# Moving the last 24 gathered dot products from the routing's expert layer into the second expert layer, and spreading the others over the routing

## The reference, cut to what matters

```python
def block(xb):
    qy = (xb @ w_query).reshape(n_tok, PEER_HEADS, 2, half)
    s1 = einsum('nhd,hkd->nhk', qy[:, :, 0], sub_keys_1)      # 8 heads, 128 keys each side
    s2 = einsum('nhd,hkd->nhk', qy[:, :, 1], sub_keys_2)
    v1, i1 = top_k(s1, 16)
    v2, i2 = top_k(s2, 16)
    cand = v1[..., :, None] + v2[..., None, :]
    cidx = i1[..., :, None] * 128 + i2[..., None, :]
    top_s, pos = top_k(cand, 16)                               # 16 experts per head and token
    eidx = take_along_axis(cidx, pos)
    gates = softmax(top_s)
    u = expert_u[eidx]
    vv = expert_v[eidx]
    act = gelu(einsum('nhkd,nd->nhk', u, xb))
    return einsum('nhk,nhkd->nd', gates * act, vv)
```

## Time and profile before

| what | us |
|---|---|
| median of 3 runs (1887.15, 1889.95, 1893.63) | 1889.95 |
| the profiled execution, as a run | 1888.03 |
| its span, first to last instruction | 1885.9 |
| PE busy in the span | 1706.8 (91%) |
| DVE busy | 1407.3 (75%) |
| ACT busy | 690.9 (37%) |
| POOL busy | 478.0 (25%) |

### The profile page before, as it was taken

The page is one execution under the profiler, slowest core; times in us unless marked ns, Lnnn a source line. Parts: engine busy times, 40 slices in busy tenths (PEclk is TensorE's granted clock), DMA queues, the critical chain, the costliest instruction groups (busy, mean ns, idle before and its releaser), DMA issues. The chain is left out here.

```text
span 1885.9 us, 28850 instructions
## 1 busy us (share of the span) xinstructions
PE 1706.8 (91%) x9877; PEld 1555.0 (82%) x9877; DVE 1407.3 (75%) x2542; ACT 690.9 (37%) x1048; POOL 478.0 (25%) x340
## 2 busy tenths in 40 slices
PE   6997778886979999998969998997799999999997
PEld 3875576544758899998869998997799999999996
DVE  4777766877332388798899998975688788788786
ACT  4763222235142233423324443432333333333333
POOL 1000000000110367776713332344122222222220
PEclk8998998897989999998979999999899999999999
DMA  3221000000223358876858887899799999999993
GB/s 109 96 96 38 1 1 35 23 1 24 66 78 101 135 164 270 280 241 222 288 164 318 327 322 257 323 378 379 272 331 355 345 343 359 331 360 339 344 357 109
DMA packets 149135, 404.54 MB, mean 215 GB/s; under 512 B 14100, under 2 KB 71700, under 8 KB 145592
## 3 DMA queue, kind: packets, MB, share of 16 engines
q1 hardware_dynamic: 108728, 243.99, 38.8%
q0 software_dynamic: 36864, 134.23, 18.8%
q10 hardware_dynamic: 3456, 25.17, 3.3%
HBM read 350.90 MB, written 52.44 MB: 214 GB/s over the span
## 5 line engine op out<-in xcount | busy, mean ns | idle before, releaser
L1579 PE MATMUL bank<-h_hi,rt_u_hi 128*128 128x384 f32 x1024 | 356.5, 348 | 34.3 <-DVE rt_u_lo L1369 24.8
L1711 PE MATMUL bank<-va_w_hi,va_v_hi 128*128 128x384 f32 x1024 | 343.4, 335 | 16.2 <-DVE va_w_lo L1676 16.2
L1581 PE MATMUL bank<-h_hi,rt_u_lo 128*128 128x384 f32 x1024 | 347.0, 339 | 0.0
L1580 PE MATMUL bank<-h_lo,rt_u_hi 128*128 128x384 f32 x1024 | 346.9, 339 | 0.0
L1713 PE MATMUL bank<-va_w_hi,va_v_lo 128*128 128x384 f32 x1024 | 343.2, 335 | 0.0
L1712 PE MATMUL bank<-va_w_lo,va_v_hi 128*128 128x384 f32 x1024 | 343.1, 335 | 0.0
L1297 ACT ACTIVATE rt_u_hi<-raw 128x1024 fp32r<-128x1024 f32 x128 | 135.6, 1060 | 410.8 <-PE bank L1581 343.8
L1662 ACT ACTIVATE va_v_hi<-raw 128x1024 fp32r<-128x1024 f32 x128 | 135.7, 1060 | 345.3 <-PE bank L1713 341.2
L1340 POOL DMA_INDIRECT h<-u_rows_dram,own_experts x128 | 169.0, 1320 | 280.5 <-DVE rt_waste L1376 270.1
L1787 POOL DMA_INDIRECT qy<-v_dram,own_experts x128 | 130.7, 1021 | 409.5 <-DVE va_own L1696 403.5
L1676 DVE TENSOR_TENSOR va_v_lo<-raw,va_v_hi 128x1024 fp32r<-128x1024 f32 x128 | 156.8, 1225 | 103.2 <-ACT va_v_hi L1662 98.3
(11 more groups left out here) (323 smaller groups left out, 2703.2 us busy)
## 6 DMA issues: line engine op xcount, KB each, us to landing
raw<-u_dram SPq DMA_DIRECT2D x128, 512.0 KB
raw<-v_dram SPq DMA_DIRECT2D x128, 512.0 KB
active_scratch<-rt_act SPq DMA_DIRECT2D x128, 192.0 KB
gates_scratch<-early ACTq DMA_DIRECT2D x24, 1024.0 KB, 7.1
early<-gates_scratch SPq DMA_DIRECT2D x16, 1536.0 KB
early<-active_scratch SPq DMA_DIRECT2D x128, 192.0 KB
in_raw<-w_in_dram SPq DMA_DIRECT2D x22, 512.0 KB, 3.5
query_raw<-w_query_dram SPq DMA_DIRECT2D x16, 512.0 KB, 3.5
```

The lines of the kernel that those rows point to most:

```text
L1579: mm(bank, u_hi[:, j % 2, cols], hi[:, c, 0:TD], start=c == 0, stop=False)
L1580: mm(bank, u_hi[:, j % 2, cols], lo[:, c, 0:TD], start=False, stop=False)
L1581: last = mm(bank, u_lo[:, j % 2, cols], hi[:, c, 0:TD], start=False, stop=c == DC - 1)
L1711: mm(bank, v_hi[:, j, cols], w_hi[:, j, :], start=start, stop=False)
```

## The change

The last 24 columns of `dots` (104 to 127) are no longer computed in the route stage but in the first 96 slabs of the value stage, one for every four slabs, in front of the `own` step of slabs 0, 4, 8 and so on. Phase 2 of the route has 8 dots (one per two slabs) instead of 32. Their rows of `u` are gathered by GpSimd in the value stage, one behind every fourth `v` gather. Since PSUM is needed there, ScalarE copies `h_tok` at the end of the route to a part of `qy` (SBUF); the ring `y` and the tiles `dots`, `waste`, `gelu_own` and `gate_own` are allocated for both stages. Gelu and the product with the gates run twice: for columns 0 to 103 at the end of the route, for 104 to 127 in slabs 96 and 104 of the value stage. For that, the last four groups of eight slabs are written out behind the loop on every engine but TensorE.

In phase 0 the number of dots in a body stays 16: eight in `best_keys` as before, then one after every second head of `best_pairs` (four) and four inside `list_experts` (`own_dot`).

```diff
+EARLY_DOTS = 104
...
-    DOTS = (16, 16, 32)
+    DOTS = (16, 16, 8)
...
-                act.wait_ge(s["dot"], SLOTS)
-                a(gelu_own[:], dots[:], ACT.Gelu).then_inc(s["gelu"], 1)
+                act.wait_ge(s["placed"], 2 * BODY * BODIES[1])
+                act.wait_ge(dot, EARLY_DOTS)
+                a(ahead["h_tok"], h_tok[:], ACT.Copy).then_inc(s["kept"], 1)
+                a(gelu_own[:, 0:EARLY_DOTS], dots[:, 0:EARLY_DOTS], ACT.Gelu).then_inc(s["gelu"], 1)
+                act.wait_ge(s["kept"], 1)
...
-                for k in range(START[1] - BODY, SLOTS):
+                for k in range(START[1] - BODY, EARLY_DOTS + RING):
                     gather(k)
...
-                        if i:
-                            early_dot(DOTS[0] * (i - 1) + PH + h)
+                        if i and h % 2:
+                            early_dot(DOTS[0] * (i - 1) + PH + h // 2)
...
+                    own_dot = lambda q: early_dot(DOTS[0] * (i - 1) + PH + PH // 2 + q) if i else None
+                    own_dot(0)
                     both = prod.rearrange("p s n a -> p (s n) a")
                     halve(both, 8)
                     halve(both, 4)
+                    own_dot(1)
...
                                          flat(iota[:, 0:PTOP]), ALU.is_equal))
+                    own_dot(2)
...
                     link(d.tensor_reduce(out[:, 2, :], prod[:, 0, :, 0:4], AX.X, ALU.add))
+                    own_dot(3)
...
-        def run(eng, body):
+        def run(eng, body, between=None):
+
             body(0, 0, True)
             body(0, 1, False)
-            with eng.Fori(1, N // 16) as i:
+            with eng.Fori(1, LATE // 16) as i:
                 body(i, 0, False)
                 body(i, 1, False)
+            for u in range(LATE // 8, N // 8):
+                if between:
+                    between(u)
+                body(u // 2, u % 2, False)
...
+                def gelus(u):
+                    if u == LATE // 8:
+                        act.wait_ge(dot, SLOTS)
+                        late = slice(EARLY_DOTS, SLOTS)
+                        nc.scalar.activation(gelu_own[:, late], dots[:, late], ACT.Gelu).then_inc(late_gelu, 1)
...
                     ahead["gather"]([k])
+                    m = EARLY_DOTS + RING + (k - RING) // 4
+                    if k % 4 == 0 and m < SLOTS:
+                        ahead["gather_u"](m)
...
+                        if k % 4 == 0 and not (isinstance(i, int) and 8 * u >= LATE):
+                            r = 2 * z + k // 4
+                            column = EARLY_DOTS + 2 * u + k // 4
+                            dve.wait_ge(u_rows_in[r], 16 * (EARLY_DOTS // RING + i + 1))
+                            dve.wait_ge(dot, column)
+                            nc.vector.scalar_tensor_tensor(waste[:], u_ring[:, r, :], 1.0, h_tok, ALU.mult, ALU.mult,
+                                                           accum_out=dots[:, bass.ds(column, 1)]).then_inc(dot, 1)
...
+                def weights(u):
+                    if u == LATE // 8 + 1:
+                        dve.wait_ge(late_gelu, 1)
+                        late = slice(EARLY_DOTS, SLOTS)
+                        nc.vector.tensor_tensor(w_own[:, late], gelu_own[:, late], gate_own[:, late], ALU.mult).then_inc(zeroed, 1)
+                        dve.wait_ge(zeroed, 2)
...
+    def gather_u(k):
+        if k >= RING:
+            t.nc.gpsimd.wait_ge(dot, k - RING + 1)
+        t.nc.gpsimd.indirect_dma_start(
+            out=u_ring[:, k % RING, :], out_offset=None, in_=u_rows,
+            in_offset=bass.IndirectOffsetOnAxis(ap=eidx[:, k:k + 1], axis=0)).then_inc(u_rows_in[k % RING], 16)
```

More of the change, by code:

```diff
@@ L1118, in route_stage @@
     RING = 4
-    DOTS = (16, 16, 32)
+    DOTS = (16, 16, 8)
     FIRST_DOT = (0, 48, 96)
-    ld_u, keys_in = ahead["u"], ahead["keys"]
+    ld_u, keys_in, rows_in, dot = (ahead[k] for k in ("u", "keys", "u_rows", "dot"))
+    ring, dots, waste, gelu_own, gate_own = (ahead[k] for k in ("u_ring", "dots", "waste", "gelu_own", "gate_own"))
     kept_a = [t.sem(f"rt_active_stored{i}") for i in range(4)]
     sent = [t.sem(f"rt_chunk_sent{i}") for i in range(2)]
-    rows_in = [t.sem(f"rt_rows_in{i}") for i in range(RING)]
     u_high, u_low, u_low_late, first, active = (
@@ L1128, in route_stage @@
         "chain", "picked", "scores", "taken", "tops", "exps", "listed", "chosen", "turned", "slots_t", "slots",
-        "iota", "hots", "hot", "placed", "moved", "dot", "gelu")}
+        "iota", "hots", "hot", "placed", "moved", "gelu", "kept")}
     with ExitStack() as ctx:
@@ L1335, in low @@
                                             ALU.subtract).then_inc(u_low, 1)
-                def gather(k):
-                    if k >= RING:
-                        pool.wait_ge(s["dot"], k - RING + 1)
-                    nc.gpsimd.indirect_dma_start(
-                        out=ring[:, k % RING, :], out_offset=None, in_=u_rows,
-                        in_offset=bass.IndirectOffsetOnAxis(ap=eidx[:, k:k + 1], axis=0)).then_inc(rows_in[k % RING], 16)
+                gather = ahead["gather_u"]
                 for e in range(BODY + 1):
@@ L1374, in take_dot @@
                     if not (isinstance(k, int) and k == 0):
[L1375 removed]
+                        dve.wait_ge(dot, k)
                     d.scalar_tensor_tensor(waste[:], ring[:, r, :], 1.0, h_tok[:], ALU.mult, ALU.mult,
[L1377 removed]
+                                           accum_out=dots[:, bass.ds(k, 1)]).then_inc(dot, 1)
                 def early_dot(k):
@@ L1616, in value_stage @@
     gate, act_s, ring = (ahead[k] for k in ("gate", "act", "ring"))
+    u_ring, u_rows_in, dot, h_tok = (ahead[k] for k in ("u_ring", "u_rows", "dot", "h_tok"))
+    dots, waste, gelu_own, gate_own = (ahead[k] for k in ("dots", "waste", "gelu_own", "gate_own"))
+    late_gelu = t.sem("va_late_gelu")
+    SLOTS = PH * PTOP
+    LATE = 4 * (SLOTS - EARLY_DOTS)
     v_high, v_low, gated, w_high, w_low, second, added, zeroed = (
@@ L1664, in eight @@
                         nc.scalar.activation(w_hi[:, par, :], w[:, par, :], ACT.Copy).then_inc(w_high, 1)
-                run(act, eight)
+                def gelus(u):
[3 more added lines that the diff above has]
+                        nc.scalar.activation(gelu_own[:, late], dots[:, late], ACT.Gelu).then_inc(late_gelu, 1)
+                run(act, eight, gelus)
             @block.gpsimd
@@ L1699, in _ @@
                 dve.wait_ge(zeroed, 1)
-                run(dve, eight)
+                def weights(u):
[4 more added lines that the diff above has]
+                        dve.wait_ge(zeroed, 2)
+                run(dve, eight, weights)
             @block.tensor
@@ L1783, in peer_buffers @@
     rows_in = [t.sem(f"va_rows_in{i}") for i in range(RING)]
+    u_ring = y[:].rearrange("p (r c) t -> p r (c t)", r=RING)
+    u_rows_in = [t.sem(f"rt_rows_in{i}") for i in range(RING)]
+    dot = t.sem("rt_dot")
+    def gather_u(k):
[4 more added lines that the diff above has]
+            in_offset=bass.IndirectOffsetOnAxis(ap=eidx[:, k:k + 1], axis=0)).then_inc(u_rows_in[k % RING], 16)
     def gather(ks):
@@ L1793, in peer_buffers @@
             "g": [t.sem(f"va_gates_loaded{i}") for i in range(2)], "rows": rows_in, "ring": ring, "gather": gather,
+            "u_ring": u_ring, "u_rows": u_rows_in, "dot": dot, "gather_u": gather_u,
+            "h_tok": qy[:, 12:14, :].rearrange("p c t -> p (c t)"), "waste": sb("own_waste", [P, D], BF16),
+            "dots": sb("own_dots", [P, PH * PTOP], F32), "gelu_own": sb("own_gelu", [P, PH * PTOP], F32),
+            "gate_own": sb("own_gates", [P, PH * PTOP], F32),
             "gate": early[:, 0:gates].rearrange("p (z c k n) -> p z c k n", z=2, c=TD // CH, k=8),
@@ L1843, in first_tiles @@
                     sp.dma_start(raw[:, e, :], a["u"][e]).then_inc(ahead["u"][e], 16)
-            with ExitStack() as route:
-                y = route.enter_context(nc.sbuf_tensor("h2", [P, DC, T], F32))
-                project_stage(t, "query", a["w_query"], 2 * PH, x, V_LN2, hi, lo, lambda i: qy[:, i, :], y=y, then=first_tiles)
-                route_stage(t, qy, y, hi, lo, raw, early, a["u"], a["u_rows"], a["gates"], a["active"], a["v"], eidx, w_own,
-                            ahead)
+            project_stage(t, "query", a["w_query"], 2 * PH, x, V_LN2, hi, lo, lambda i: qy[:, i, :], y=y, then=first_tiles)
+            route_stage(t, qy, y, hi, lo, raw, early, a["u"], a["gates"], a["active"], a["v"], eidx, w_own, ahead)
             value_stage(t, raw, a["v"], a["gates"], a["active"], w_own, ahead)
```

16 lines of the change are left out of this document (6 added, 10 removed).

## The result

The kernel after takes 1860.82 us (median of 4 runs, 1858.56 to 1863.42), the kernel before 1889.54 us (4 runs, 1887.15 to 1893.63): a ratio of 0.985 (95% interval 0.982 to 0.987), or 29 us less. The forecast was 1860 us. The span of the profiled execution is 1856.8 us, 29.1 under the 1885.9 of before; -29.5 was the sum. That the sum fits is partly luck, as the stages show: two of its terms are off by 5 and by 7.5 us, in opposite directions.

A forecast was written before the change was run, and what follows sets the result against it. TensorE was taken as the bound after the route stage, with gains only where it idles. -14 - 8.7 - 7.2 + 0.4 = -29.5 us from a 1888.0 us run gave 1858.5, stated as a 1860 us median; 8-in-10 range 1846 to 1877.

The forecast's parts named there:

- What bounds the kernel: Whole kernel: TensorE bounds after the route; time can be won in routing, the last 16 slabs and the seam.
- Routing: Slabs 16 to 63: spreading dots removes 20.0 us of waits, +3 stretching and +3 late rows come back: -14 us.
- price of 1.5 us for a `low`: Routing lists: each GpSimd `low` under a list costs VectorE 1.5 us; body 1's list becomes 26.6 us.
- 3 us for dots that meet a row just landing: Routing: now and then a dot still meets a row that is just landing; 3 us added back.
- the end of -5: Routing's least gain: a `low` costs 2.1 us and no dot ever covers it, 10.3 us more in the lists.
- GpSimd's stands: Routing: with the gather ring full GpSimd stands at a gather, 9.15 us or longer, and the `low` queued behind is late.
- Last 16 slabs: End of the first layer: 8 dots instead of 32 leave TensorE the bound, 75.4 us to 66.6 + 0.1: -8.7 us.
- Seam: Route's last matmul to the value stage's first: the queue drains earlier, 16.3 us becomes 9.1: -7.2 us.
- end of -2: Seam's least gain: the value gathers' 2.1 MB still delay the stores.
- Value stage: Second layer: 24 added dots and gathers fit in VectorE's spare time and DMA at 378 GB/s: 0, 5 us doubt.
- Rivals C and D: Value stage: C, DMA full at 360 GB/s, +20 us, 1880 (6%); D, random rows hold DMA under break-even 352, slower (4%).
- Rival B: Routing and seam: GpSimd takes the routing's gain, subtractions cost 2.1 us each, seam stays long: -16, 1874 us (13%).

The follow-up runs named there:

- e1_spread_only: The kernel before with only the new spreading of dots in `best_pairs` and `list_experts`; phase 2 keeps its 32 dots: 1870.86 us, ratio 0.991.
- e2_late_only: The kernel after with the old `best_pairs` and `list_experts`, so only the move of 24 dots to the value stage: 1879.42 us, ratio 0.995.
- e3_list_dots_last: The kernel after with each list's four dots moved from between its steps to its end: 1873.18 us, ratio 0.991.
- e7_best: e5_no_gather_at_seam with no dots in the lists, 12 a body, 20 instead of 8 in the last 16 slabs, gathers after three of four `low`s: 1870.62 us.
- e9_gathers_by_dots: e8_even_bodies with a body's twelfth gather issued after its last `low`, none after the four before it: 1849.49 us, ratio 0.978.
- e8_even_bodies: e5_no_gather_at_seam with 12 dots per list body (pairs lose theirs), 20 per chunk body, gathers after a body's first 12 `low`s: 1861.65 us.
- e4_v_first: The kernel after with GpSimd's four gathers of `v` issued ahead of phase 2's gathers of `u`: 1856.38 us, ratio 0.983.
- e5_no_gather_at_seam: e4_v_first with the gathers of `u` rows 105 to 107 also moved behind the barrier into the value stage: 1851.37 us, ratio 0.979.
- e6_extra_rows: The kernel after with 20 more 512 KB gathers in the value stage, into parts of `qy` nothing reads: 1876.59 us, ratio 0.993.

## Why the prediction was right, and where it was not

**What bounds the kernel: right.** TensorE idle in the routing, in the last 16 slabs and at the seam was the whole account. e1_spread_only and e2_late_only split the gain into 19.1 and 10.6 us, together 1.0 more than the whole, so neither part gives or takes anything that these runs can tell.

**Routing, -14 forecast, -19.1 measured: mechanism right, the stretching mis-sized.** The waits in front of dots fell by 24.3 - 4.2 = 20.1 us; 20.0 were forecast. What the forecast gave back for the list was too much. By the same reckoning as there (length less 12.8 us, and less 5.1 for the dots), the three lists are stretched by 3.5, 4.8 and 1.6 us, together 9.8, against 12.1 in before: -2.3 where +3 was charged. The forecast had 8.7 us for body 1's list alone. Its price of 1.5 us for a `low` was an average over work that isn't alike. VectorE's timeline in body 1's list of after shows where it is paid:

```profile
768.35 3.30 DVE L1441 TENSOR_TENSOR early<-early,rt_step 128x2048 bf16<-128x2048 bf16 x1
771.57 1.21 DVE L1443 TENSOR_TENSOR early<-early,rt_rows 128x2048 bf16<-128x2048 bf16 x1
772.82 1.22 DVE L1371 SCALAR_TENSOR_TENSOR own_waste<-h,bank 128x1024 bf16<-128x1024 f32 x1
...
782.21 2.16 DVE L1459 TENSOR_TENSOR early<-early,rt_second 128x2048 bf16<-128x2048 bf16 x1
```

A step is stretched only if it meets GpSimd at the wrong moment: L1441 by 2.1 us over its 1.23, L1459 by about 0.9, L1443 not at all; the dots keep their 1.22. GpSimd pays in the same meetings, in the same list:

```profile
767.79 2.77 POOL L1334 TENSOR_TENSOR rt_u_lo<-raw,rt_u_hi 128x1024 fp32r<-128x1024 f32 x1 [0.59 <-ACT rt_u_hi L1294]
770.71 1.76 POOL L1824 DMA_INDIRECT h<-u_rows_dram,own_experts  x1
```

Its `low` takes 2.77 us there and 2.39 otherwise, its gather 1.76 and 0.95 otherwise. (The Trainium skill, SBUF — State Buffer, "SBUF: two separate sides", has VectorE and GpSimd share one pair of ports, which a GpSimd instruction, or a VectorE one with two inputs in SBUF, locks for its whole length. The trace agrees in kind: 3.30 us is 1.23 and most of one `low`, and the dots, which have one input in PSUM, keep their time.) How much body 1's list is stretched depends on what stands between its steps: 3.5 us with dots between them, 5.3 with the dots behind them (e3_list_dots_last), 7.3 with none (e7_best), and 5.9 in e9_gathers_by_dots, where the dots are as in after but GpSimd gets there at other moments. The three bodies have -20.1 from waits and -2.3 in the lists, which is 3.3 us more than the 19.1 measured. The forecast kept 3 us for dots that meet a row just landing; that term was nothing, since the 4.2 us of waits that are left are the 4.3 that it had already left in. The 3.3 us lie between the lists, and not in waits. Half of them is in the timelines: the product that makes the gates (`rt_out`, L1473) took 1.03 and 2.35 us where it had taken 0.29 twice, `rt_soft` (L1418) took 0.9 us more in the three bodies, and `rt_cand` (L1405) 2.1 less, together 1.6. So the stretching moved in part from the list to the steps beside it. The other half comes from the reckoning, which charges 1.3 us for each of the twelve moved dots, where successive starts in these rows show some 1.16: at that price the lists' stretching falls by 0.9 instead of 2.3 us, and 1.8 us stand against the 1.6 of the timelines. (In the prediction the end of -5 is also off: by its own terms, 10.3 us more than -14, it is -4.)

**GpSimd's stands: seen, and undervalued.** The forecast treated them as a sign that gathers run ahead, and as cover that would be lost. e3_list_dots_last and e8_even_bodies show the other side: a gather issued ahead of its buffer holds the `low`s behind it, and that cost TensorE 13.5 and 20.1 us, against 3.2 in after and 1.4 where the order of gathers follows that of the dots.

**Last 16 slabs, -8.7: right.** Measured -8.7, in after and in e2_late_only alike, with TensorE busy throughout.

**Seam, -7.2 forecast, nothing measured: this step failed.** The sentence that failed is that GpSimd's five gathers "end about 3 us after TensorE, before SP is done". The issuing does end there (1286.75 against TensorE's 1285.35). But the barrier wants GpSimd's queue drained, and it drained 12.3 us after the start of the last gather. SP did come earlier, 7.2 us behind the end of the last matmul against 12.4, as forecast in kind; GpSimd took its place. e4_v_first and e5_no_gather_at_seam show the gathers as the cause by moving nothing else: the seam's wait goes 16.5, 10.3, 6.4 us, and the time 1860.8, 1856.4, 1851.4 us. Of the 10.1 us of wait that went, the drain had held 5.6; the other 4.5 is the store of SP, delayed by the gathers beside it (4.0 of these went in e4_v_first, which only changes their order). That is what the prediction's own end of -2 said ("the value gathers' 2.1 MB still delay the stores"): without the drain the term would have come to some -5, not -7.2. The trace of before held the warning: GpSimd's drain ended only 3.4 us before SP's. What the drain waits for stays open; the runs show only that it follows the start of the last gather, by 9.8 to 12.9 us in all eleven kernels.

**Value stage, 0 forecast, -1.2 measured: right, with less room than claimed.** In after 24 dots on VectorE cost nothing and TensorE never stops. DMA moved 378 GB/s, as worked out. But the 0 is not safe: in the profiles of e2_late_only, e4_v_first and e5_no_gather_at_seam TensorE does stop in this stage, once, once and twice, for 2.1, 2.6 and 2.7 us in all, where a slab of `v` and an `active` tile landed late (ScalarE waits 4.7, 6.4 and 4.5 us for the slab), and in these three the kernel takes 3 to 4 us longer behind the seam than in after. Rivals C and D had 360 and 352 GB/s; 389 were moved here (e6_extra_rows), so they were wrong about the number and right about the mechanism: at 378 it shows now and then, with 3% more traffic all the time. (The 358 GB/s for a core of the Trainium skill, DMA: Bandwidth & Descriptors, "Where 436 GB/s comes from", is not what bounds this kernel running alone: it moved 378 without a stop, and 389 at most over 300 us.)

**Rival B**, GpSimd taking the gain, was wrong for the routing and right for the seam, by the stores that it named for a part, and for the greater part by the drain that it did not. **The other signs**: no wait before slab 64 over 19 us (13.4), that slab near 944 (939.4, better by the routing's 5 us), GpSimd's waits at gathers at most 5 us (4.4), slabs 112 to 127 in 67 us (66.5), no wait of VectorE in the pairs or the lists, DMA near 378: all as said. A seam near 9 us: not.

## What to carry to other kernels

Before a barrier, look at when each engine's queue has drained, not when it issued its last instruction; an engine that issues gathers should issue its last one well before the end, here 10 to 13 us. Where a queue mixes work that others wait for with transfers that wait for a buffer, order the transfers by the time their buffers come free, or the work behind them is late. And a gain that comes from filling gaps is worth a split into its parts: here two errors of 5 and 7.5 us largely cancelled in the total, and the one at the seam, once found, was worth another 9 us.

## What the runs showed of the hardware

- GpSimd's drain at a barrier ended 12.3, 11.1 and 9.8 us after the start of its last indirect DMA of 512 KB (after 1285.81, e4_v_first 1280.21, e5_no_gather_at_seam 1260.06).
- A store of 192 KB landed 6.4 us after its issue beside four such indirect DMAs (after), and 2.3 and 1.9 us after it without them (e4_v_first, e5_no_gather_at_seam).
- An elementwise VectorE step on two bf16 inputs of 2,048 columns took 3.30 us beside GpSimd's subtraction and 1.23 us without it; a multiply with a sum over 1,024 elements, with one input in PSUM, kept 1.22 us in both cases. GpSimd's own DMA issue took up to 1.77 us beside some of such steps, and 0.95 us beside the multiply with a sum.
- One core, alone, moved 389 GB/s over 300 us with all its DMA engines full, in slab loads of 4 KB rows and gathers of 4 KB rows together.
